# Short FP32 matmuls cut into four column groups, and three steps put in another place, in a two-block FP32 kernel on one core

## The reference, cut to what matters

```
def ssd_scan(x, dt, A, Bm, Cm):
    ...
    X = (x * dt[..., None]).reshape(bsz, nc, L, SSD_GROUPS, r, SSD_HEAD_DIM)
    a_cum = jnp.cumsum(a, axis=-1)
    ...
    decay_in = jnp.exp(jnp.where(tril, seg, -jnp.inf))
    cb = jnp.einsum('bclgn,bcsgn->bcgls', Cc, Bc)
    y_diag = jnp.einsum('bcgls,bcgrls,bcsgrp->bclgrp', cb, decay_in, X)
    ...
    y_off = jnp.einsum('bclgn,bcgrpn,bcgrl->bclgrp', Cc, prev, jnp.exp(a_cum))
```

## Time and profile before

| | |
|---|---|
| median of 3 runs | 1618.67 us (1617.04 to 1618.92) |
| the profiled execution | 1619.15 us |
| its span, first to last instruction | 1617.4 us, so 1.75 us lie outside the span |
| TensorE's mean granted clock | 0.999 |
| PE busy | 99% of the span |
| DVE, ACT, POOL busy | 67%, 44%, 11% |

### The profile page before, as it was taken

The page is one execution under the profiler, slowest core; times in us unless marked ns, Lnnn a source line. Parts: engine busy times, 40 slices in busy tenths (PEclk is TensorE's granted clock), DMA queues, the critical chain, the costliest instruction groups (busy, mean ns, idle before and its releaser), DMA issues.

```text
span 1617.4 us, 19268 instructions
## 1 busy us (share of the span) xinstructions
PE 1596.0 (99%) x7599; PEld 1318.8 (82%) x7599; DVE 1079.1 (67%) x1494; ACT 711.1 (44%) x1018; POOL 181.7 (11%) x263
## 2 busy tenths in 40 slices
PE   9999999999999999999999999999999999999998
PEld 7878777788888888888788887888888888878888
DVE  7745788668484865656744568445566976878857
ACT  6524375545252523414662155441334443443444
POOL 0001145100000000014500245000000000000000
PEclk9999999999999999999999999999999999999999
DMA  5224231165757522331132221323248347344221
GB/s 190 83 79 145 85 131 53 63 224 130 234 130 234 130 104 79 131 130 52 53 105 78 83 75 53 130 104 105 81 147 265 110 124 236 97 149 156 103 106 53
DMA packets 32890, 195.06 MB, mean 121 GB/s; under 512 B 4321, under 2 KB 6817, under 8 KB 11297
## 3 DMA queue, kind: packets, MB, share of 16 engines
q1 hardware_dynamic: 25056, 160.20, 27.6%
q0 software_dynamic: 2880, 20.97, 6.9%
q10 hardware_dynamic: 4864, 12.66, 2.2%
HBM read 187.50 MB, written 6.32 MB: 120 GB/s over the span
## 4 chain that ended last, share of the span: by engine, by line
PE 88%; DVE 6%; issue 2%; ACT 2%; DMA 1%; POOL 1%; DVEq 0%; POOLq 0%
PE bank L759 20%; PE bank L761 20%; PE bank L760 20%; PE bank L1181 4%; PE bank L1182 3%; PE bank L1183 3%; PE bank L807 3%; PE bank L809 3%; PE bank L808 3%; PE bank L993 1%; PE bank L767 1%; DMA w_raw<-in_parts 1%; PE bank L978 1%; PE bank L1099 1%; DVE w_lo L1957 1%
## 5 line engine op out<-in xcount | busy, mean ns | idle before, releaser
L759 PE MATMUL bank<-a_hi,w_hi 128*128 128x512 f32 x1160 | 457.3, 394 | 0.6 <-DVE x L2021 0.6
L761 PE MATMUL bank<-a_hi,w_lo 128*128 128x512 f32 x1160 | 452.8, 390 | 0.0
L760 PE MATMUL bank<-a_lo,w_hi 128*128 128x512 f32 x1160 | 452.1, 390 | 0.0
L1367 ACT ACTIVATE w_hi<-w_raw 128x2048 fp32r<-128x2048 f32 x95 | 181.3, 1909 | 187.7 <-DMA w_raw<-in_strips 185.8
L761 PEld LDWEIGHTS bank<-a_hi,w_lo 128*128 128x128 f32 x1160 | 218.0, 188 | 46.2
L759 PEld LDWEIGHTS bank<-a_hi,w_hi 128*128 128x128 f32 x1160 | 218.4, 188 | 44.7 <-issue 1.4
L760 PEld LDWEIGHTS bank<-a_lo,w_hi 128*128 128x128 f32 x1160 | 218.4, 188 | 43.1 <-issue 0.2
L1942 DVE TENSOR_TENSOR w_lo<-w_raw,w_hi 128x2048 fp32r<-128x2048 f32 x92 | 211.1, 2296 | 54.9 <-ACT w_hi L1367 54.8
L1181 PE MATMUL bank<-w_hi,t_hi 128*128 128x512 f32 x280 | 109.3, 390 | 1.7 <-DVE w_lo L2361 1.7
L1182 PE MATMUL bank<-w_lo,t_hi 128*128 128x512 f32 x280 | 109.0, 389 | 0.0
L1183 PE MATMUL bank<-w_hi,t_lo 128*128 128x512 f32 x280 | 109.0, 389 | 0.0
(11 more groups left out here) (368 smaller groups left out, 2660.0 us busy)
## 6 DMA issues: line engine op xcount, KB each, us to landing
w_raw<-in_strips SPq DMA_DIRECT2D x107, 1024.0 KB, 4.9
a_part<-in_parts SPq DMA_DIRECT2D x25, 1024.0 KB, 7.6
a_part<-in_parts POOLq DMA_DIRECT2D x20, 1024.0 KB, 9.8
spare<-in_parts SPq DMA_DIRECT2D x5, 1024.0 KB, 15.1
spare<-in_strips SPq DMA_DIRECT2D x5, 1024.0 KB, 4.8
seg_in<-cum_kept ACTq DMA_DIRECT2D x16, 256.0 KB, 3.4
x_kept<-x ACTq DMA_DIRECT2D x2, 2048.0 KB, 8.8
x<-x_kept SPq DMA_DIRECT2D x2, 2048.0 KB, 9.4
```

Of the source, the lines that this page charges most:

```text
L759: mm(ps[:, :], w_hi[slot][:, k, cols], hi[:, k, :], start=(k == 0), stop=False)
L760: mm(ps[:, :], w_hi[slot][:, k, cols], lo[:, k, :], start=False, stop=False)
L761: return mm(ps[:, :], w_lo[slot][:, k, cols], hi[:, k, :], start=False, stop=(k == kt - 1))
L1367: run(w_hi[j], w_raw[j], ACT.Copy).then_inc(hi_split, 1)
```

## The change

A helper `by_columns` splits a matmul with 128 stationary columns into four with 32, which write the output partitions 0 to 31, 32 to 63, 64 to 95 and 96 to 127. It is used in the decay products, both column sums, `turn_small` and the products with `tri` and `ones`. `turn_xs(8)` and `turn_xs(9)` are put behind the first output tile of qk, and `turn_small(0)` one tile later; ACT's `keep_small(0)` goes ahead of its last two `keep_xs`. On SP, part 6 is loaded behind part 3 in down0 and down1, and waits until part 3 has landed.

```diff
--- before.py
+++ after.py
@@ -567,14 +567,16 @@
 
             def other_parts(g):
 
-                for i in (5, 6):
-                    sp_eng.wait_ge(strip_split, FIRST[SEVEN[g]] + A_STAGE[i] + 1)
-                    load_stage(g, i)
+                sp_eng.wait_ge(strip_split, FIRST[SEVEN[g]] + A_STAGE[5] + 1)
+                load_stage(g, 5)
 
                 if SERIES[g]:
 
                     sp_eng.wait_ge(unit_done, 2 * FIRST[SEVEN[g]] + 2)
                     sp_eng.dma_start(flat(strip_source(g, 3)), part_of((0, 0), g)).then_inc(part_loaded[2], 16)
+                    sp_eng.wait_ge(part_loaded[2], plain_count(g, 3))
+                sp_eng.wait_ge(strip_split, FIRST[SEVEN[g]] + A_STAGE[6] + 1)
+                load_stage(g, 6)
                 sp_eng.wait_ge(strip_split, FIRST[SEVEN[g]] + 5)
                 sp_eng.dma_start(flat(spare), d["strips"][STRIP_AT[FIRST[NEXT[g]]]]).then_inc(spare_loaded, 16)
 
@@ -735,6 +737,12 @@
         @block.tensor
         def _(pe):
             mm, tr = nc.tensor.matmul, nc.tensor.transpose
+
+            def by_columns(dst, stationary, moving):
+
+                for g in range(0, P, 32):
+                    last = mm(dst[g:g + 32, :], stationary[:, g:g + 32], moving, start=True, stop=True)
+                return last
 
             def bank_free(phase, j, fills=0):
 
@@ -906,7 +914,7 @@
             def column_sums(where, at, total):
 
                 for t in range(TT):
-                    last = mm(where[:, at + t:at + t + 1], total[:, t * P:(t + 1) * P], ones[:, 0:1], start=True, stop=True)
+                    last = by_columns(where[:, at + t:at + t + 1], total[:, t * P:(t + 1) * P], ones[:, 0:1])
                 return last
 
             def spread(norm, where=STAT[0], tok=norm_tok):
@@ -935,8 +943,7 @@
                 pe.wait_ge(small_ready, 6)
                 pe.wait_ge(sp_exp, 3 * which + 1)
                 for t in range(TT):
-                    last = mm(bank[7][:, t * 16:(t + 1) * 16], small_t[:, t * P:(t + 1) * P], sel.bitcast(F32),
-                              start=True, stop=True)
+                    last = by_columns(bank[7][:, t * 16:(t + 1) * 16], small_t[:, t * P:(t + 1) * P], sel.bitcast(F32))
                 last.then_inc(small_done, 1)
 
             def attention(call, phase, dense, lead=None):
@@ -1047,19 +1054,20 @@
             keep_clock(bank[7], T, 19)
             first_strips()
             stream("xbc", feature_k, A, within=within_xbc, begin=3)
-            turn_xs(8)
             small_columns(0)
-            turn_xs(9)
 
 
             def after_qk(j):
-                if j == 1:
+                if j == 0:
+                    turn_xs(8)
+                    turn_xs(9)
+                if j == 2:
                     turn_small(0, "mix1")
                 if j != 5:
                     return
                 pe.wait_ge(sp_step, SP_A)
-                mm(bank[6][:, 0:64], tri, sp["a"], start=True, stop=True)
-                mm(bank[6][:, 64:128], ones, sp["a"], start=True, stop=True)
+                by_columns(bank[6][:, 0:64], tri, sp["a"])
+                by_columns(bank[6][:, 64:128], ones, sp["a"])
                 for c in range(TT):
                     last = mm(bank[7][0:16, c * P:(c + 1) * P], sp["a"][:, c * 16:(c + 1) * 16], tri, start=True, stop=True)
                 last.then_inc(cum_done, 1)
@@ -1096,8 +1104,8 @@
                     for g in range(GROUPS):
                         pe.wait_ge(mixed_ready, 2 * c + g + 1)
                         for h in range(8):
-                            last = mm(bank[5 + g][:, h * HEAD:(h + 1) * HEAD], decay[:, 8 * g + h, :],
-                                      x_dt[:, (8 * g + h) * HEAD:(8 * g + h + 1) * HEAD], start=True, stop=True)
+                            last = by_columns(bank[5 + g][:, h * HEAD:(h + 1) * HEAD], decay[:, 8 * g + h, :],
+                                              x_dt[:, (8 * g + h) * HEAD:(8 * g + h + 1) * HEAD])
                         if g == 0:
                             last.then_inc(y_done, 1)
                             fill(p0 + 10, p0 + 12)
@@ -1322,7 +1330,7 @@
             def half_sums(at, total, half):
                 for t in range(2):
                     tok = slice((2 * half + t) * P, (2 * half + t + 1) * P)
-                    last = mm(STAT[1 - half][:, at + t:at + t + 1], total[:, tok], ones[:, 0:1], start=True, stop=True)
+                    last = by_columns(STAT[1 - half][:, at + t:at + t + 1], total[:, tok], ones[:, 0:1])
                 return last
 
             def half_spread(where, half):
@@ -1513,6 +1521,10 @@
                     dst = b_tok[:, :, (m - 8) * P:(m - 7) * P]
                 run(dst, src, ACT.Copy).then_inc(xs_ready, 1)
 
+            def keep_small(k):
+                act.wait_ge(small_done, 2 * k + 1)
+                run(small_t, bank[6][:, :], ACT.Copy).then_inc(sp_exp, 1)
+
             def first_tap(m):
                 act.wait_ge(dve_evac, EVAC0["xbc"] + m + 1)
                 if m >= 2:
@@ -1532,22 +1544,19 @@
                     first_tap(m)
                 if m:
                     silu(m - 1)
-                if m >= 4:
+                if 4 <= m < NXBC:
                     keep_xs(m - 4)
                 if 2 <= m < NXBC and m % 2 == 0:
                     hi(FIRST["xbc"] + m // 2 + 2)
+            keep_small(0)
+            keep_xs(8)
             keep_xs(9)
             hi(FIRST["qk"] + 2)
-
-            def keep_small(k):
-                act.wait_ge(small_done, 2 * k + 1)
-                run(small_t, bank[6][:, :], ACT.Copy).then_inc(sp_exp, 1)
 
             def log_exp(k):
                 act.wait_ge(sp_step, SP_A * k + 3)
                 run(sp["e"], sp["na"], ACT.Exp).then_inc(sp_exp, 1)
 
-            keep_small(0)
             run(exp_a, heads1[:, 1, :], ACT.Exp).then_inc(cum_act, 1)
             log_exp(0)
             hi(FIRST["qk"] + 3)
```

## The result

The changed kernel takes 1607.21 us (median of five executions, 1607.03 to 1607.68) beside 1618.92 us (five of before in the same job, 1617.04 to 1619.13): a ratio of 0.9932, interval 0.9921 to 0.9943. The prediction was 1607.0.

A forecast was written before the change was run, and what follows sets the result against it. PE, busy for 99% of the span, was taken as the bound. Savings of 4.1 + 2.6 + 3.6 + 1.3 = 11.6 us from 1619.15, less 0.48 for the median, gave 1607.0 us, range 1604.8 to 1612.3.

The forecast's parts named there:

- A: Scan's decay products: four column groups cut a group from 1.78 to 1.22 us, 4.1 us in all.
- The wait of chunk 2: Second decay group of chunk 2: PE will wait some 0.4 us for DVE's `decay`.
- Rival 1: Narrow bursts: a pace of starts above 0.023 us holds throughout, so decay groups gain nothing; 1613.6 us, chance 0.10.
- rival 3: Decay products: the four column groups take turns, a group costs 3.8 us, kernel slower at about 1630; chance 0.07.
- B: Column sums, turnings of the 16 columns, `tri` and `ones` in column groups: 2.6 us saved, between 1 and 3.5.
- C: Turnings of tiles 8 and 9 behind qk's first tile: 2.0 us idle and 1.6 us half clock go, 3.6 us.
- 3.4 us at half rate cost 1.6 us: PE from 84.2 to 87.65: the half clock behind the idle time costs 1.6 us, expected to go.
- The sum 11.6: Whole kernel: savings of 4.1 + 2.6 + 3.6 + 1.3 us, taken from the profiled 1619.15.
- Rival 2: A saving is eaten: clock falls anyway, part 6 late, or scan waits for `seg_in`; 1609.5 to 1612, chance 0.16.
- D: down0 and down1: part 3 ahead of part 6 removes ACT's waits of 0.27 and 1.11 us; 1.3 us saved.
- Part 6 is late next: down1: part 6 lands at 1422, ACT's step ends at about 1434, DVE takes it a microsecond before 1435.09; just holds.
- The stated lower end: Forecast range's lower end, 1604.8 us: upper bounds of the savings, 13.3, and a microsecond for the unseen.

The follow-up runs named there:

- e3: Kernel before with only the decay products split into four column groups of 32 stationary columns: 1613.76 us, ratio 0.9976.
- e5: Kernel before with only the column sums, `turn_small` and the `tri` and `ones` products in four column groups: 1615.86 us, ratio 0.9987.
- e9: Changed kernel with the turnings of tiles 8 and 9, `turn_small(0)` and `keep_small` back in their old places: 1609.16 us, ratio 0.9948.
- e1: Kernel before with only the turnings of tiles 8 and 9, `turn_small(0)` and `keep_small(0)` moved: 1615.24 us, ratio 0.9983.
- e4: Kernel before with only the decay products split, into two column groups of 64 stationary columns: 1614.57 us, ratio 0.9979.
- e6: Kernel before with only SP's order changed in down0 and down1: part 3, wait for its landing, then part 6: 1617.06 us, ratio 0.9995.
- e7: Kernel before with only part 6 issued right behind part 3 in down0 and down1, without waiting for its landing: 1616.91 us, ratio 0.9991.
- e10: Changed kernel with the C·B products (128 moving columns) in four column groups too: 1608.09 us, ratio 0.9941.
- e11: Changed kernel with the scan's products of 512 moving columns in four column groups too: 1607.37 us, ratio 0.9937.

## Why the prediction was right

**A, decay products: 4.1 predicted, 4.27 measured.** The group costs 1.23 (1.22 predicted), its round 0.056 as predicted. The wait of chunk 2 came, from the chain that the prediction named, and is 0.30 instead of 0.4. Rival 1, a pace of starts of 0.023 or more, and rival 3 fall: 64 and 128 starts in a row go at 0.014, 32 with one column at 0.0084, and e3 beside e5 shows that with 64 columns the round is limited by its columns. The rule in the Trainium skill, TensorE: Matmul & The Clock Gate, on the 56 ns gap, that matmuls never start less than about 25 ns apart, does not hold for short matmuls in different column groups here; the rows decide. Within one column group no two starts came closer than 0.03 us in these runs, so whether it holds there was not tried.

**B: 2.6 predicted, 2.7 measured.** The round of one column is 0.034, not 0.045, so each lone sum or call of `turn_small` saved 0.33 to 0.38 instead of 0.32, and the pair at 680 1.13 instead of 1.0. `tri` and `ones` brought 0.15 (0.2), the halves at the end under 0.1 of the span.

**C: 3.6 predicted, 3.6 in the trace, 2.0 in more than half of the executions.** The mechanism of the idle time was right, and e9 and e1 measure it (1.95 us; 1615.24 against the 1617.4 of before's executions with the full clock is 2.2). Wrong was "3.4 us at half rate cost 1.6 us" as something that each execution pays: it is in 34 of 81, and in the profiled one. The sum 11.6 fits the medians (11.7) because four of the five executions of before beside the change were of that kind. Against before's executions at 1617.4 the change saves 10.2 us. Rival 2's part "the clock falls all the same" did not come: the changed kernel's executions lie within 0.65 us.

**D: 1.3 predicted, 1.6 measured.** It was sized from ACT's waits (1.11 and 0.27). What counted was how much later DVE got its strip: its step on `w_raw` in down1 has 0.58 us of idle time ahead of it, 1.80 before, and 1.22 is the step measured. The wait of PE at L1181, 1.7 us and now 0.1, had the size of this trace all along; other profiles without part D have 1.0 to 1.6 there, so 1.6 is near the upper end of what D is worth. Part 6 is late next, as said, and holds: ACT's step for it begins at 1420.23 and ends at 1422.15, and DVE takes it at 1424.00.

**The start and the sum.** The start cost 0.79 us that no term had, from the spread between executions. So the mechanisms were right, but that the forecast lies 0.2 us from the median is in part luck: the terms measured 12.2 instead of 11.6, the start took most of the difference back, and before's five executions were mostly of the slower kind. The stated lower end is also misadded: 13.3 and a microsecond below 1618.67 is 1604.4, not 1604.8. Nothing hangs on it.

The parts alone add up to the same: by steps 3.6 + 4.4 + 2.7 + 1.6 = 12.3 for 12.2 in the change. They don't hinder one another, except in chunk 2 (0.27 with all, 0.44 with the decay products alone).

## What to carry to other kernels

Plain FP32 matmuls with 1, 16 and 64 moving columns went at one pace here, 0.11 us, that of the load of 128 stationary columns. Column groups take it away, at 0.3 us for getting into the mode and out. So keep such matmuls together in one run of them, and leave alone those whose columns take as long as the load (128 and 512 gained nothing). Two groups of 64 are nearly as good as four of 32 at 64 moving columns. A feature of one trace (here 1.55 us at half clock) is not yet one of every execution: look for two heaps in the times before a median is set against it. And size a stall from the wait of the engine that bounds the kernel, not from the wait further up the chain.

## What the runs showed of the hardware that I had not expected

- After the same 2.04 us of idle time TensorE's granted clock fell to 1.2 GHz for some 3.4 us in the profiled executions of three kernels (before, e4, e5) and stayed at 2.4 in those of four (e3, e6, e7, e9); with 2.97 us both kinds are still seen by the times. The fall goes with when the clock rose at the start: it came where the opening burst took 6.44 to 6.75 us, 78.51 us behind the rise each time, and not where it took 6.06 and 6.18 or 7.08 and 7.46. Why is open.
- Matmuls with 32 stationary columns, in turn on four column groups, start 0.0084 us apart with one moving column or 16, and 0.014 with 64, over as many as 128 in a row. Their loads go with them: PEld has 64 in 0.94 us, so loads for different column groups overlap.
- Coming out of the narrow records costs more than getting in: the dense matmul behind a decay group is 0.50 long for 0.39, and the next starts 0.34 later where 0.23 is usual; ahead of the group the spacing is 0.32, 0.09 more than usual. A pass of 128 moving columns gains nothing by groups (e10), and one of 512 nothing either (e11).
